# B products of the state space stage issued later, and list addresses computed between the expert selections

## The chip, the cores and the metric

One Trainium2 chip, of which the kernel uses one core. The metric is device microseconds for one execution; the kernel before took 1758.97 us (median of three runs, 1758.9 to 1761.51). The engines run side by side and wait for each other through semaphores: TensorE (PE; its weight loads are PEld), VectorE (DVE), ScalarE (ACT), GpSimd (POOL) and SyncE (SP), whose queue starts most transfers.

## The reference, cut to what matters

One decoder layer over 512 tokens of width 1024, float32 throughout:

```python
proj = h @ w_in[l]                       # u, q, k, v, indexer, merge gates
y_ssm = s5_branch(u, ...)                # 32 groups x 16 channels, 64 complex states, a scan over 512 positions
y_att = dsa_branch(...) @ w_attn_proj    # 8 heads, each query keeps 128 keys chosen by an indexer
mix = (g_ssm * y_ssm + g_att * y_att) @ w_o
h = layer_norm(ALPHA * h + mix, ...)
# experts
top_val, top_idx = lax.top_k(h @ w_router + b_router, 4)     # 4 of 32
# every expert: swiglu(x @ w_up + b_up) @ w_down + b_down, times the token's gate, summed over the 4
h = layer_norm(ALPHA * h + ffn, ...)
```

## The kernel before, in words

Every engine has one list of instructions in an order written out by hand; a `wait_ge` holds the whole list of its engine. Two stretches of these lists are touched.

**The state space stage.** The 32 groups are 16 blocks of 128 complex states (j = 0 to 15), taken in pairs. `bu(p)` (line 1474) is TensorE's B product of pair p: eight matmul records with 32 rows, into four PSUM banks. It waits until VectorE has taken the pair before it out of these banks (`s_bufree >= 2 * p`, which the fourth product of block 2p - 1 gives, line 1032). `s5(j)` on VectorE is twelve instructions (lines 1029 to 1045): four products with sines and cosines, two sums, two scans, four products; the last gives `s_st`. `ymm(q)` (line 1488) is the C product of four blocks and waits for `s_st >= 4 * q + 4`. Between them TensorE computes the tiles of the input projection (`tile`, line 1442 for most, 1423 for v, eight products of 128x128 by 512 each, shown as 16 records). Which product stands where is given by two tables over the tile index i of the loop at line 1497, and within one i the C product comes first:

```python
bu_at = {1: 1, 4: 2, 7: 3, 10: 4, 13: 5, 15: 6, 18: 7}
y_at = {6: 0, 12: 1, 17: 2}
```

After tile i = 20 TensorE goes on with `dots(0)` (line 1524), the first indexer products, which wait for `s_bufree >= 16`: the fourth product of the last block, j = 15. Gate tiles (line 1515) and further dots follow, until attention begins at `qk` (line 1556). A tile is copied out by ScalarE (`take`, line 738), in one list with its sines (`trigs`).

**The routing stage.** For each of four tiles t of 128 tokens: `w_out(t)` on TensorE, layer norm on VectorE (lines 1168 to 1182), transposes and router product (`route`, lines 1626 to 1640; ScalarE copies the transposes, line 860), the selection on VectorE (lines 1187 to 1204; ScalarE's two exponentials stand in the middle), `place(t)` (each token's position within its expert), then on VectorE `first_addresses(t)`: positions, the marks of the rows of expert 0 (`in_first`) and four list addresses for each token. GpSimd's `write_first(t)` writes the tokens' numbers with four indirect DMAs (line 586) to the list `first_list`. When all 16 writes have landed (`s_scat`) SyncE loads the list as `slots` (line 460), and only then issues the weight loads beyond the eighth part; VectorE waits for `slots` at line 1302, in front of its split `lo(-1, 7)`. `first_rows(t)` (line 1665) sums the rows of expert 0 straight into PSUM, a tile at a time, so that the first expert can begin before any list is read.

**The first expert** is `up_part(-1, p + 4, p)` for p = 0 to 7: three products for each of four banks (lines 1715 to 1717), of a weight part that SyncE loads, ScalarE rounds (`hi`, line 832) and VectorE takes the rest of (`lo`, line 1163). Part p needs `lo(-1, p + 4)`. Behind p = 1 stand the products of the first two tiles' gated biases (line 1694), whose sums VectorE takes in `sums` (line 1255) after `lo(-1, 7)`. The remaining experts run in a loop over blocks of 96 rows.

Of the kernel before, what the change touches and what calls it, by code (L numbers as in the profile page):

```python
# [16 lines left out]
ACT = mybir.ActivationFunctionType  # L17
ALU = mybir.AluOpType
# [7 lines left out]
P = 128  # L26
# [59 lines left out]
def build(nc, a, out):  # L86
# [14 lines left out]
    with ExitStack() as ctx:  # L101
# [555 lines left out]
        def _(act):  # L657
# [182 lines left out]
            for t in range(TT):  # L840
                act.wait_ge(s_var, TT + t + 1)
                s.activation(rsx[:, t, 0:1], mvx[:, t, 1:2], ACT.Sqrt, bias=eps[:, 0:1]).then_inc(s_rstd, 1)
                if t == 1:
                    act.wait_ge(s_bs, 1)
                    step(s.activation(bias3[third, :], braw_b[third, :], ACT.Copy))
                    s.activation(brem[third, :], bias3[third, :], ACT.Copy).then_inc(s_bc, 1)
                if t == 2:
                    step(s.activation(bias3[second, :], braw_b[second, :], ACT.Copy))
                    act.wait_ge(s_bs, 2)
                    s.activation(bias3[third, :], braw_b[third, :], ACT.Copy).then_inc(s_b3l, 1)  # L850
                if t == 3:
                    for c in range(4, 6):
                        hi(-1, c)
                act.wait_ge(s_h1, t + 1)
                act.dma_start(h1_rows.rearrange("(t p) d -> p t d", p=P)[:, t, :], h[:, t, :]).then_inc(s_h1row, 16)
                for r in range(2):
                    act.wait_ge(s_h1T, 2 * t + r + 1)
                    if t > 0:
                        act.wait_ge(s_lgt, t)
                    s.activation(hT1[:, 4 * r:4 * r + 4, :], ps[6 + r][:, :].rearrange("p (k q) -> p k q", k=4),  # L860
                                 ACT.Copy).then_inc(s_h1e, 1)
                act.wait_ge(s_v8, t + 1)
                s.activation(all_exp[:, t, :], lg[:, :], ACT.Exp, bias=gneg[:, 0:1])
                s.activation(gates[:, t, :], rt8[:, t, 0:TOPK], ACT.Exp, bias=gneg[:, 0:1],
                             accum_out=gsum[:, 0:1]).then_inc(s_ge, 1)
            def T_hi(dst, half, job, bank):

                act.wait_ge(s_tr, job + 1)
                s.activation(dst[:, 4 * half:4 * half + 4, :].rearrange("p k t -> p (k t)"), ps[bank][:, 0:4 * BLK],
                             ACT.Copy).then_inc(s_thi, 1)  # L870
# [10 lines left out]
            s.activation(gdT, ps[1][0:NE, :], ACT.Copy).then_inc(s_gdTe, 1)  # L881
# [54 lines left out]
        def _(dve):  # L936
# [209 lines left out]
            def first_addresses(t):  # L1146

                dve.wait_ge(s_pos, t + 1)
                step(d.tensor_copy(pos[:, t, :], ps[1][:, 0:NE]))
                d.tensor_scalar(in_first[:, t, :], tcol[:, 0:BLK], pos[:, t, 0:1], chosen[:, t, 0:1], ALU.is_equal,  # L1150
                                ALU.mult).then_inc(s_inf, 1)
                ad, picked = adw[:, t, 0, :], adw[:, t, 1, :]
                step(d.scalar_tensor_tensor(ad, pos[:, t, :], float(NE), tcol[:, 0:NE], ALU.mult, ALU.add))
                for k in range(TOPK):
                    step(d.scalar_tensor_tensor(picked, tcol[:, 0:NE], rif[:, t, k:k + 1], ad, ALU.is_equal, ALU.mult,
                                                accum_out=addr[:, t, k:k + 1]))
                d.tensor_copy(addr_i[:, TOPK * t:TOPK * t + TOPK], addr[:, t, :]).then_inc(s_adr, 1)
                dve.wait_ge(s_adr, t + 1)
# [8 lines left out]
            for t in range(TT):  # L1167
# [15 lines left out]
                if t > 0:  # L1183
                    first_addresses(t - 1)
                if t == TT - 1:
                    lo(-1, 4)
# [18 lines left out]
            first_addresses(TT - 1)  # L1205
# [90 lines left out]
            for half in range(2):  # L1296
                T_lo(x_lo, x_hi, half, half, 2 + half)
            lo(-1, 5)
# [3 lines left out]
            dve.wait_ge(s_slots, 16)  # L1302
            next_token(1)
            for c in range(7, 15):
                lo(-1, c)
                if c == 7:
                    dve.wait_ge(s_h1row, 16 * TT)
                    sums(0)
# [79 lines left out]
        def _(pe):  # L1388
# [105 lines left out]
            bu_at = {1: 1, 4: 2, 7: 3, 10: 4, 13: 5, 15: 6, 18: 7}  # L1494
# [131 lines left out]
            def route(t):  # L1626
                pe.wait_ge(s_h1, t + 1)
                for r in range(2):
# [5 lines left out]
                    ins.then_inc(s_h1T, 1)  # L1634
                pe.wait_ge(s_h1e, 2 * t + 2)
# [7 lines left out]
            def place(t):  # L1643

                pe.wait_ge(s_chosen, t + 1)
                if t > 0:
                    pe.wait_ge(s_adr, t)
# [5 lines left out]
            for t in range(TT):  # L1653
# [3 lines left out]
                if t > 0:  # L1657
                    route(t - 1)
# [12 lines left out]
            place(TT - 2)  # L1671
# [3 lines left out]
            first_rows(0)  # L1675
            first_rows(1)
            route(TT - 1)
# [8 lines left out]
            for t in range(TT):  # L1686
                ins = tr(ps[1][0:NE, P * t:P * t + P], all_exp[:, t, :], ident[:, :])
# [72 lines left out]
            pe.wait_ge(s_adr, TT)  # L1760
            pe.wait_ge(s_gdTe, 1)
            for p in range(8):
                up_part(-1, p + 4, p)
                if p == 1:
                    pe.wait_ge(s_bias, 64)
# [57 lines left out]
```

## Time and profile before

| | us |
|---|---|
| median of 3 runs | 1758.97 (1758.9 to 1761.51) |
| profiled execution | 1764.82, span 1763.10 |
| PE busy | 1686.9 (96%) |
| DVE busy | 1499.1 (85%) |
| ACT busy | 1063.4 (60%) |
| POOL busy | 467.5 (27%) |
| mean granted TensorE clock | 0.973 of full |

In the timeline a row is a start, a time, an engine, a line of the kernel, the operation, out<-in with shapes, and how many instructions are merged into it; in brackets stands how long the engine was idle before it and whose event ended this. An idle engine costs something only where the chain of waits runs through it.

### The profile page before, as it was taken

The page shows a single profiled execution, that of the slowest core. Times are in us where ns is not written, and L with a number is a line of the kernel's source. Part 1 is how long each engine was busy: PE and PEld are TensorE (multiplying, and loading weights), DVE is VectorE, ACT ScalarE, POOL GpSimd, SP SyncE. Part 2 cuts the span into 40 slices and gives each one's busy share as a digit, 9 for nine tenths or more (in the row PEclk, how much of TensorE's full clock was granted, in tenths as well). Part 3 has the DMA queues.
Part 4 walks back from the last instruction along what each step waited for, and adds up shares of the span by engine and source line. Part 5 has one row for each costly group of instructions (what it writes and reads, how often), then busy time and mean ns, then how long its engine had stood idle before and what let it go on. Part 6 is the DMA issues. An engine that isn't in the chain of part 4 may idle for free.

```text
span 1763.1 us, 22201 instructions
## 1 busy us (share of the span) xinstructions
PE 1686.9 (96%) x7129; PEld 1107.8 (63%) x7129; DVE 1499.1 (85%) x1710; ACT 1063.4 (60%) x1016; POOL 467.5 (27%) x298
## 2 busy tenths in 40 slices
PE   5899999999997999999999999999999999999996
PEld 2333344476576577777777777777777777777763
DVE  5999877555568799999999999999999999999995
ACT  4332222365445477777777777777777777777771
POOL 4855000064334111223121212222222212121210
PEclk9999899998998899999999999999999999999998
DMA  5111122110316789999999999999999999999973
GB/s 172 48 51 48 48 76 92 58 48 39 120 45 227 304 308 369 368 366 366 368 382 358 368 365 378 361 365 360 373 365 369 364 371 374 363 355 373 382 293 104
DMA packets 91901, 464.76 MB, mean 264 GB/s; under 512 B 21289, under 2 KB 21405, under 8 KB 42616
## 3 DMA queue, kind: packets, MB, share of 16 engines
q1 hardware_dynamic: 80240, 441.67, 65.9%
q0 software_dynamic: 9776, 18.41, 4.3%
q10 hardware_dynamic: 1848, 4.24, 0.7%
q8 instruction: 17, 0.28, 0.1%
q14 instruction: 20, 0.16, 0.0%
HBM read 454.15 MB, written 18.53 MB: 268 GB/s over the span
## 4 chain that ended last, share of the span: by engine, by line
PE 87%; DVE 9%; ACT 2%; issue 1%; DMA 0%; ACTq 0%; DVEq 0%
PE ps L1715 20%; PE ps L1717 20%; PE ps L1716 20%; PE ps L1515 6%; PE ps L1701 3%; PE ps L1442 2%; PE ps L1437 2%; PE ps L1723 2%; PE ps L1423 2%; PE ps L1431 1%; PE ps L1623 1%; PE ps L1622 1%; PE ps L1621 1%; PE ps L1576 1%; PE ps L1433 1%
## 5 line engine op out<-in xcount | busy, mean ns | idle before, releaser
L1163 DVE TENSOR_TENSOR w_lo<-raw,w_hi 128x2048 fp32r<-128x2048 f32 x384 | 874.1, 2287 | 76.3 <-ACT w_hi L832 76.2
L832 ACT ACTIVATE w_hi<-raw 128x2048 fp32r<-128x2048 f32 x384 | 737.0, 1920 | 244.6 <-PE ps L1717 244.2
L1715 PE MATMUL ps<-w_hi,x_hi 128*96 128x512 f32 x1024 | 415.9, 406 | 0.0
L1717 PE MATMUL ps<-w_lo,x_hi 128*96 128x512 f32 x1024 | 404.7, 395 | 0.0
L1716 PE MATMUL ps<-w_hi,x_lo 128*96 128x512 f32 x1024 | 404.4, 395 | 0.0
L1715 PEld LDWEIGHTS ps<-w_hi,x_hi 128*96 128x96 f32 x1024 | 169.3, 165 | 67.5 <-issue 1.5
L1717 PEld LDWEIGHTS ps<-w_lo,x_hi 128*96 128x96 f32 x1024 | 166.7, 163 | 71.1 <-issue 0.2
L1715 PE MATMUL ps<-w_hi,a_hi 128*96 128x512 f32 x512 | 204.6, 400 | 5.7 <-DVE a_lo L1261 5.7
L1716 PEld LDWEIGHTS ps<-w_hi,x_lo 128*96 128x96 f32 x1024 | 167.0, 163 | 64.0 <-issue 0.2
L1716 PE MATMUL ps<-w_hi,a_lo 128*96 128x512 f32 x512 | 201.8, 394 | 0.0
L604 POOL DMA_INDIRECT gate_now<-gate_rows,row_now x32 | 79.8, 2495 | 458.8 <-DVE tok_out L1291 443.7
L1717 PE MATMUL ps<-w_lo,a_hi 128*96 128x512 f32 x512 | 201.5, 394 | 0.0
L612 POOL DMA_INDIRECT sum_rows<-far,tok_out x31 | 77.2, 2489 | 335.7 <-ACT far L918 335.7
L1442 PE MATMUL ps<-ring 128*128 128x512 f32 x256 | 120.1, 629 | 2.5 <-ACT ring L686 2.0
L1515 PE MATMUL ps<-ring 128*128 128x512 f32 x256 | 111.5, 595 | 0.0
L1715 PEld LDWEIGHTS ps<-w_hi,a_hi 128*96 128x96 f32 x512 | 83.0, 162 | 39.2 <-issue 5.8
L1717 PEld LDWEIGHTS ps<-w_lo,a_hi 128*96 128x96 f32 x512 | 83.1, 162 | 36.3
L1716 PEld LDWEIGHTS ps<-w_hi,a_lo 128*96 128x96 f32 x512 | 83.3, 163 | 33.4
L1442 PEld LDWEIGHTS ps<-ring 128*128 128x128 f32 x256 | 50.8, 202 | 71.6 <-issue 69.3
L596 POOL DMA_INDIRECT scr<-h_rows,tok_now x32 | 70.5, 2205 | 81.3 <-DVE tok_now L1285 74.3
L1515 PEld LDWEIGHTS ps<-ring 128*128 128x128 f32 x256 | 48.2, 190 | 61.5 <-issue 61.2
L918 ACT ACTIVATE far<-ps,gate_now 96x512 f32<-96x512 f32 x64 | 40.3, 678 | 42.7 <-PE ps L1717 42.7
(323 smaller groups left out, 2034.6 us busy)
## 6 DMA issues: line engine op xcount, KB each, us to landing
raw<-in_w_up SPq DMA_DIRECT2D x256, 1024.0 KB, 8.0
raw<-in_w_down SPq DMA_DIRECT2D x128, 1024.0 KB, 9.4
ring<-in_w_in SPq DMA_DIRECT2D x9, 2048.0 KB, 7.8
ring<-in_w_glu SPq DMA_DIRECT2D x4, 1024.0 KB, 6.3
ring<-in_w_o SPq DMA_DIRECT2D x2, 2048.0 KB, 11.7
h<-in_x SPq DMA_DIRECT2D x4, 512.0 KB, 4.9
ring<-in_w_attn_proj SPq DMA_DIRECT2D x1, 2048.0 KB, 8.9
h_rows<-h ACTq DMA_DIRECT2D x4, 512.0 KB, 3.6
```

Source lines behind the costliest of these rows:

```text
L596: g.indirect_dma_start(xg[:, :], None, h1_rows, bass.IndirectOffsetOnAxis(ap=tok_now[:, 0:1], axis=0), bounds_check=last_tok, oob_is_err=F ...
L604: g.indirect_dma_start(gate_now[:, :], None, gate_rows, bass.IndirectOffsetOnAxis(ap=row_now[:, 0:1], axis=0), bounds_check=last_row, oob_ ...
L612: g.indirect_dma_start(sum_rows, bass.IndirectOffsetOnAxis(ap=tok_out[:, 0:1], axis=0), ysb.rearrange("p a b -> p (a b)"), None, bounds_ch ...
L832: s.activation(hi_of(c)[:, :], raw_of(c), ACT.Copy).then_inc(s_hi, 1)
L918: s.activation(ysb[:, r, :], ps[4 + r][0:BLK, :], ACT.Copy, scale=gate_now[:, 0:1]).then_inc(s_ysb, 1)
L1163: d.tensor_tensor(lo_of(c)[:, :], raw_of(c), hi_of(c)[:, :], ALU.subtract).then_inc(s_lo, 1)
L1442: ins = mm(o[:, :], w[:, k, c:c + P], hT[:, k, :], start=k == 0, stop=k == KD - 1)
L1515: ins = mm(ps[n % 2][:, :], gate_weights(g)[:, k, :], hT[:, k, :], start=k == 0, stop=k == KD - 1)
L1701: ins = tr(ps[bank][:, BLK * k:BLK * k + BLK], cols(k), ident[0:BLK, 0:BLK])
L1715: mm(o, xh, hi_of(c)[:, col], start=start, stop=False)
L1716: mm(o, xl, hi_of(c)[:, col], start=False, stop=False)
L1717: return mm(o, xh, lo_of(c)[:, col], start=False, stop=stop)
```

## The change

Five edits, in the diff below, cut where a loop body is only made into a function:

- `bu_at`: the third pair comes one tile later (4 to 5), the seventh two (15 to 17), the last one (18 to 19).
- VectorE: `norm1(3)` moves in front of `first_marks(1)` and `choose(2)`; the addresses of tiles 1 and 2 are computed together, behind `choose(2)`, those of tile 3 behind the x splits; each time by five instructions over all choices and tiles, in place of six for a tile. `lo(-1, 4)` moves behind the last marks, and the wait for `slots` behind `lo(-1, 7)`.
- ScalarE: `std(3)` moves in front of the exponentials of tile 2, the split `hi(-1, 4)` in front of those of tile 3.
- TensorE: the router's transposes and products of tile 3 move up, around `place(2)`; `place` waits for `s_inf` (marks) and no longer for `s_adr` (addresses).
- The gates' transposes go to bank 4 in place of bank 1, and their wait moves from in front of the first expert to behind p = 1; the wait for `s_adr >= TT` goes.

```diff
...
+            std(2)
+            step(s.activation(bias3[second, :], braw_b[second, :], ACT.Copy))
+            act.wait_ge(s_bs, 2)
+            s.activation(bias3[third, :], braw_b[third, :], ACT.Copy).then_inc(s_b3l, 1)
+            rows_off(2)
+            keep_hT1(2)
+            std(3)
+            gate_exps(2)
+            rows_off(3)
+            keep_hT1(3)
+            hi(-1, 4)
+            gate_exps(3)
+            hi(-1, 5)
...
-            def first_addresses(t):
+            def first_marks(t):
                 dve.wait_ge(s_pos, t + 1)
                 step(d.tensor_copy(pos[:, t, :], ps[1][:, 0:NE]))
                 d.tensor_scalar(in_first[:, t, :], tcol[:, 0:BLK], pos[:, t, 0:1], chosen[:, t, 0:1], ALU.is_equal,
                                 ALU.mult).then_inc(s_inf, 1)
-                ad, picked = adw[:, t, 0, :], adw[:, t, 1, :]
-                step(d.scalar_tensor_tensor(ad, pos[:, t, :], float(NE), tcol[:, 0:NE], ALU.mult, ALU.add))
-                for k in range(TOPK):
-                    step(d.scalar_tensor_tensor(picked, tcol[:, 0:NE], rif[:, t, k:k + 1], ad, ALU.is_equal, ALU.mult,
-                                                accum_out=addr[:, t, k:k + 1]))
-                d.tensor_copy(addr_i[:, TOPK * t:TOPK * t + TOPK], addr[:, t, :]).then_inc(s_adr, 1)
-                dve.wait_ge(s_adr, t + 1)
+            def first_addresses(t0, t1):
+                shape = [P, t1 - t0, TOPK, NE]
+                ad = adw[:, t0:t1, 0, :]
+                picked = part_lo[:, 0:(t1 - t0) * TOPK * NE].rearrange("p (t k e) -> p t k e", k=TOPK, e=NE)
+                step(d.scalar_tensor_tensor(ad, pos[:, t0:t1, :], float(NE),
+                                            tcol[:, 0:NE].unsqueeze(1).to_broadcast([P, t1 - t0, NE]), ALU.mult, ALU.add))
+                step(d.tensor_tensor(picked, tcol[:, 0:NE].unsqueeze(1).unsqueeze(1).to_broadcast(shape),
+                                     rif[:, t0:t1, 0:TOPK].unsqueeze(3).to_broadcast(shape), ALU.is_equal))
+                step(d.tensor_tensor(picked, picked, ad.unsqueeze(2).to_broadcast(shape), ALU.mult))
+                step(d.reduce_sum(addr[:, t0:t1, :], picked, AXL.X))
+                d.tensor_copy(addr_i[:, TOPK * t0:TOPK * t1], addr[:, t0:t1, :].rearrange("p t k -> p (t k)"))\
+                    .then_inc(s_adr, t1 - t0)
+                dve.wait_ge(s_adr, t1)
...
+            norm1(0)
+            choose(0)
+            norm1(1)
+            first_marks(0)
+            first_addresses(0, 1)
+            choose(1)
+            norm1(2)
+            norm1(3)
+            first_marks(1)
+            choose(2)
+            first_marks(2)
+            first_addresses(1, TT - 1)
+            choose(3)
+            first_marks(3)
+            lo(-1, 4)
...
             for half in range(2):
                 T_lo(x_lo, x_hi, half, half, 2 + half)
+            first_addresses(TT - 1, TT)
             lo(-1, 5)
             lo(-1, 6)
             tables()
             final = dve.value_load(etab_i[0:1, NB:NB + 1], min_val=NE - 1, max_val=NB - 2)
-            dve.wait_ge(s_slots, 16)
-            next_token(1)
             for c in range(7, 15):
                 lo(-1, c)
                 if c == 7:
+                    dve.wait_ge(s_slots, 16)
+                    next_token(1)
                     dve.wait_ge(s_h1row, 16 * TT)
                     sums(0)
...
-            bu_at = {1: 1, 4: 2, 7: 3, 10: 4, 13: 5, 15: 6, 18: 7}
+            bu_at = {1: 1, 5: 2, 7: 3, 10: 4, 13: 5, 17: 6, 19: 7}
...
                 if t > 0:
-                    pe.wait_ge(s_adr, t)
+                    pe.wait_ge(s_inf, t)
...
-            place(TT - 2)
             pe.wait_ge(s_wofree, 6)
             for half in range(2):
                 mm(ps[2 + half][:, 0:4 * BLK], ones_b[:, :], none_b[:, :], start=True, stop=False)
             first_rows(0)
+            route_T(TT - 1)
+            place(TT - 2)
+            route_lg(TT - 1)
             first_rows(1)
-            route(TT - 1)
             first_rows(2)
             place(TT - 1)
             first_rows(3)
@@ -1684,7 +1731,7 @@
 
...
-                ins = tr(ps[1][0:NE, P * t:P * t + P], all_exp[:, t, :], ident[:, :])
+                ins = tr(ps[4][0:NE, P * t:P * t + P], all_exp[:, t, :], ident[:, :])
...
-            pe.wait_ge(s_adr, TT)
-            pe.wait_ge(s_gdTe, 1)
             for p in range(8):
                 up_part(-1, p + 4, p)
                 if p == 1:
+                    pe.wait_ge(s_gdTe, 1)
                     pe.wait_ge(s_bias, 64)
                     gated_biases(0)
```

## Rows read from the trace of the kernel before

**Rows 1.** The page: busy time of TensorE, and the chain by engine.

```profile
PE 1686.9 (96%) x7129; PEld 1107.8 (63%) x7129; DVE 1499.1 (85%) x1710; ACT 1063.4 (60%) x1016; POOL 467.5 (27%) x298
...
PE 87%; DVE 9%; ACT 2%; issue 1%; DMA 0%; ACTq 0%; DVEq 0%
```

**Rows 2.** Timeline of TensorE, state space stage: start us, us, instructions, idle before.

```profile
59.72 20.87 PE L1442 MATMUL ps<-ring 128*128 128x512 f32 x48
84.67 3.08 PE L1474 MATMUL ps<-uT,ring 32*128 32x512 f32 x8 [4.09 <-DVE scr L1032]
...
124.28 7.11 PE L1442 MATMUL ps<-ring 128*128 128x512 f32 x16 [0.44 <-ACT wi L734]
132.14 1.99 PE L1474 MATMUL ps<-uT,ring 32*128 32x512 f32 x8 [0.75 <-ACT ring L738]
...
160.54 14.00 PE L1442 MATMUL ps<-ring 128*128 128x512 f32 x32
179.83 3.79 PE L1474 MATMUL ps<-uT,ring 32*128 32x512 f32 x8 [5.28 <-DVE scr L1032]
...
210.22 1.99 PE L1474 MATMUL ps<-uT,ring 32*128 32x512 f32 x8
212.13 14.00 PE L1423 MATMUL ps<-ring 128*128 128x512 f32 x32
```

**Rows 3.** Chain of waits: the C product of blocks 8 to 11.

```profile
199.66 3.57 PE ps L1488 x32
```

**Rows 4.** Busy time by stretch: time, PE, PEld, DVE, ACT, POOL, clock, DMA, GB/s.

```profile
84.67:92.24 7.57, 7.57 (x14) 2.91 (x15) 7.40 (x6) 0.66 (x2) 6.42 (x5) 0.55 0.00 0
179.83:187.84 8.01, 8.01 (x13) 3.08 (x14) 7.70 (x10) 1.16 (x3) 0.00 (x0) 0.50 0.00 0
226.07:349.63 123.56, 123.56 (x337) 53.29 (x336) 84.00 (x189) 29.86 (x48) 1.53 (x4) 1.00 0.22 77
```

**Rows 5.** Timeline of VectorE, state space stage.

```profile
131.31 0.69 DVE L1032 TENSOR_TENSOR scr<-ps,scr 128x512 f32<-128x512 f32 x1
...
186.59 0.69 DVE L1029 TENSOR_TENSOR scr<-ps,scr 128x512 f32<-128x512 f32 x1
...
212.25 0.69 DVE L1029 TENSOR_TENSOR scr<-ps,scr 128x512 f32<-128x512 f32 x1 [5.24 <-PE ps L1474]
...
224.21 0.69 DVE L1032 TENSOR_TENSOR scr<-ps,scr 128x512 f32<-128x512 f32 x1
```

**Rows 6.** Timeline of TensorE, routing and first expert.

```profile
541.48 1.07 PE L1632 MATMUL ps<-ident,h 128*128 128x128 f32 x8
...
569.12 1.03 PE L1723 MATMUL ps<-bias,pick 96*96 96x512 bf16 x4 [2.49 <-ACT scr L881]
...
589.60 0.39 PE L1715 MATMUL ps<-w_hi,x_hi 128*96 128x512 f32 x1
```

**Rows 7.** Timeline of VectorE, routing and first expert.

```profile
548.50 1.41 DVE L1171 SCALAR_TENSOR_TENSOR h<-h,ps 128x512 f32<-128x512 f32 x2
...
553.49 1.29 DVE L1181 SCALAR_TENSOR_TENSOR h<-h,rsx,gb 128x1024 f32<-128x1024 f32 x1
...
556.76 2.29 DVE L1163 TENSOR_TENSOR w_lo<-raw,w_hi 128x2048 fp32r<-128x2048 f32 x1
...
567.17 4.48 DVE L1163 TENSOR_TENSOR w_lo<-raw,w_hi 128x2048 fp32r<-128x2048 f32 x2
...
578.95 0.15 DVE L1284 COPY slot_now<-slots 96x1 int32<-96x1 int32 x1 [2.83 <-DMA slots<-first_list]
```

**Rows 8.** Timeline of GpSimd: four of the sixteen list writes.

```profile
544.48 0.98 POOL L586 DMA_INDIRECT first_list<-code,addr_i  x1 [7.83 <-DVE addr_i L1157]
...
557.50 2.41 POOL L586 DMA_INDIRECT first_list<-code,addr_i  x1 [8.18 <-DVE addr_i L1157]
...
567.27 5.24 POOL L586 DMA_INDIRECT first_list<-code,addr_i  x1 [0.31 <-issue]
572.81 0.98 POOL L586 DMA_INDIRECT first_list<-code,addr_i  x1 [0.30 <-issue]
```

More of the change, by code:

```diff
@@ L839, in _, with std, rows_off, keep_hT1 @@
             s.activation(brem, bias3[:, :], ACT.Copy).then_inc(s_bc, 1)
-            for t in range(TT):
+            def std(t):
                 act.wait_ge(s_var, TT + t + 1)
                 s.activation(rsx[:, t, 0:1], mvx[:, t, 1:2], ACT.Sqrt, bias=eps[:, 0:1]).then_inc(s_rstd, 1)
[L843 to L853, printed above, removed]
+            def rows_off(t):
                 act.wait_ge(s_h1, t + 1)
                 act.dma_start(h1_rows.rearrange("(t p) d -> p t d", p=P)[:, t, :], h[:, t, :]).then_inc(s_h1row, 16)
+            def keep_hT1(t):
                 for r in range(2):
@@ L861, in _, with gate_exps @@
                                  ACT.Copy).then_inc(s_h1e, 1)
+            def gate_exps(t):
                 act.wait_ge(s_v8, t + 1)
@@ L865, in _ @@
                              accum_out=gsum[:, 0:1]).then_inc(s_ge, 1)
+            std(0)
+            rows_off(0)
+            keep_hT1(0)
+            gate_exps(0)
+            std(1)
+            act.wait_ge(s_bs, 1)
+            step(s.activation(bias3[third, :], braw_b[third, :], ACT.Copy))
+            s.activation(brem[third, :], bias3[third, :], ACT.Copy).then_inc(s_bc, 1)
+            rows_off(1)
+            keep_hT1(1)
+            gate_exps(1)
+            std(2)
[11 more added lines that the diff above has]
+            hi(-1, 5)
             def T_hi(dst, half, job, bank):
@@ L880, in _ @@
             act.wait_ge(s_gdT, 1)
-            s.activation(gdT, ps[1][0:NE, :], ACT.Copy).then_inc(s_gdTe, 1)
+            s.activation(gdT, ps[4][0:NE, :], ACT.Copy).then_inc(s_gdTe, 1)
             def sigm(t, c):
@@ L1166, in _, with norm1 @@
             dve.wait_ge(s_gb2, 32)
-            for t in range(TT):
+            def norm1(t):
                 for r in range(2):
@@ L1182, in _, with choose @@
                     .then_inc(s_h1, 1)
[L1183 to L1186, printed above, removed]
+            def choose(t):
                 dve.wait_ge(s_lgt, t + 1)
@@ L1204, in _ @@
                 dve.wait_ge(s_gd, t + 1)
-            first_addresses(TT - 1)
+            norm1(0)
[13 more added lines that the diff above has]
+            lo(-1, 4)
             cnt, more, upto_e, t0 = rw[:, 0, :], rw[:, 1, :], rw[:, 2, :], rw[:, 3, :]
@@ L1624, in w_out, with route_T @@
                     ins.then_inc(s_wo, 1)
-            def route(t):
+            def route_T(t):
                 pe.wait_ge(s_h1, t + 1)
@@ L1634, in route, with route_lg @@
                     ins.then_inc(s_h1T, 1)
+            def route_lg(t):
                 pe.wait_ge(s_h1e, 2 * t + 2)
@@ L1657, in _ @@
                 if t > 0:
-                    route(t - 1)
+                    route_T(t - 1)
+                    route_lg(t - 1)
             def first_rows(t):
```

## The prediction, written before the changed kernel was run

> **What bounds the kernel now.** I read the page first, then the chain of waits in order of time, then the timelines of both changed stretches. On the page TensorE is busy 96% of the span and makes 87% of the chain [rows 1]: only what moves TensorE can move the end, and from the first expert on nothing in the change touches the loop. So there are two questions: when does TensorE reach the indexer products (`dots(0)`, 226.07 us), behind which it is busy in 123.56 of 123.56 us [rows 4], so that every delay there is passed on; and when does it get through the first expert.
>
> In the state space stage the reader is to see two waits of TensorE for VectorE, 4.09 us before the third pair and 5.28 us before the seventh [rows 2], each followed by a stretch at a granted clock of 0.55 and 0.50, that is for the most part or wholly at the lower of its two levels, 1.2 GHz [rows 4]. These the new tables go around. But VectorE is here nearly the equal of TensorE: from 42 to 212 us its only wait worth naming is 5.24 us, for the last pair [rows 5].
>
> **The state space stage, step by step.** Units: a tile is 7.0 us (14.00 for two), a B product 1.9 (210.22 to 212.13) [rows 2], a C product 3.6 [rows 3].
>
> Third pair. Today TensorE stops at 80.6 (59.72 + 20.87) until 84.67 and then works 7.57 us at 0.55. Tile i = 5 now fills the wait: 4.1 us and 7.57 x 0.45 = 3.4 us of lost clock go, a lead of 7.5 us. The fifth pair, which did not move, cannot use it. It needs block 7's fourth product, done at 131.31 + 0.69 = 132.0 [rows 5]; VectorE's pace does not come from the third pair, which it wants only at its next block but one. Today TensorE is there at 131.4 (124.28 + 7.11) and starts at 132.14 [rows 2]; then it would be there at 124 to 125 and wait 7 us. The lead is gone, and a wait longer than either of the two that cost clock stands in its place. I charge it what these lost: 3.4, or 8.01 x 0.5 = 4.0; taken 3.7, bounds 0 and 4.0. TensorE then runs 3.7 us late.
>
> Seventh pair. Today tile i = 15 ends at 160.54 + 14.00 = 174.5. It would end at 178.2, two more tiles at 192.3, and within i = 17 the C product stands first: 195.9, B product 197.8. The wait of 5.28 and its 4.0 go, but VectorE wants the pair at 186.59 [rows 5] and gets it at 197.8: it stands 11.2 us.
>
> Last pair. From 197.8 VectorE needs, up to block 15's fourth product, what it needed from 186.59 to 224.90 (224.21 + 0.69), less the 5.24 us wait, which goes [rows 5]: 33.1, with small waits inside of some 0.2 that go too, so 32.9. Result: 230.7. TensorE after the seventh pair has two tiles, the last pair and a tile (14.1 + 1.9 + 7.0): free at 220.9. It waits 9.8 us and begins `dots(0)` at 230.7 in place of 226.07: 4.6 us late. Behind so long a wait I charge half clock again, over the short dots (1.1 us more) and part of a gate tile (about 2.2): 3.3, bounds 0 and 4.0. Sum of the stage: **+7.9 us**, bounds +0.9 (no clock lost anywhere: 4.6 - 3.7) and +8.9.
>
> Queues: the moved products issue no DMA. SyncE's chunk loads hang on tile counts; the one needed next after the moved places, at the gate tiles, is 30 us away. ScalarE's sines for block 12 and later stand in its list behind tiles that now come some 4 us later; VectorE is 11 us late by then, which hides it.
>
> **The routing stage.** Today norm 3 starts on VectorE at 548.50 because selection 2 is in front, and ends at 554.78 (553.49 + 1.29) [rows 7]; the first expert starts at 569.12 behind a 2.49 us wait for the gates' copy [rows 6]. Then norm 3 starts with the last product of `w_out(3)`, which is out when TensorE turns to transposes at 541.48 [rows 6]; the first of its two additions can go before that, so it ends at about 541.6 + 6.3 - 0.7 = 547.2, 7.6 earlier. Behind it today are the addresses of tile 2, the split `lo(-1, 4)` (2.29), selection 3, marks and addresses 3, the marked rows, the x splits and the gates' wait: 14.3 us in all. Then: marks 1, selection 2 (about 3, my estimate), two tiles' addresses (about 1.8, as well), selection 3, marks, rows, x splits; the split, most address work and the gates' wait are out of it. I put it at the same 14.2: first expert at **561.4, 7.7 us early**. Bounds: 5, if the marked rows run at half clock; 9.5, if the first part of the expert also runs at full clock, which it does not today.
>
> This gain has a second door. The fifth part of the first expert starts today at 589.60, 20.5 us after the first [rows 6], and needs `lo(-1, 8)`, which stands on VectorE behind the wait for `slots`. Today this wait ends at 578.95 [rows 7], 6.1 us after the last of 16 list writes began (572.81) [rows 8]. Now the writes: four for tile 1 begin today at 544.48. Their addresses now come with tile 2's, at about 552.9, so 12 writes begin at about 553.7, 0.98 + 0.30 = 1.28 us apart [rows 8]: 15.4 us, 569.1. And they do not run free. The write of 557.50 took 2.41 us and ended at 559.91, 0.86 after the split that ran beside it (556.76 + 2.29); that of 567.27 took 5.24 and ended 0.86 after the two splits of 567.17 (+ 4.48) [rows 7, 8]. A write beside a split ends when the split has ended. In the new order the 12 writes meet `lo(-1, 4)` (from 557.4), 5 and 6 (from 562.6) and 7 (from 572): about 2.0 + 4.5 + 2.0 us more, less what falls into gaps. The last write would begin at 574.3 to 576.8, `slots` be there at 580.3 to 582.9. I take 581.5: 2.5 us later than today, though the expert starts 7.7 earlier. Then the tokens (0.3), the first sums (1.2) and `lo(-1, 8)` (2.3): 585.3. TensorE would be ready for part five at 561.4 + 20.5 = 581.9, or 1.8 earlier if its first products run at full clock. So it starts at 585.3, 4.3 earlier than today, after a wait of 3.4 to 5.2 us, behind which the clock may fall once more (0 to 4.0; taken 2.3). What is left: **-2.0 us**, bounds +0.5 and -9.5 (the writes unhindered).
>
> The Trainium skill (SBUF — State Buffer, Who interferes with whom) has a rule that speaks otherwise: a `tensor_tensor` of VectorE with both inputs in SBUF, which the splits are, contends with GpSimd's reads alone, and descriptor generation for GpSimd's DMAs was seen not to stall beside it. By it the writes would end at 569 and 7.5 of the gain or more stay. The two writes above contradict it in this trace.
>
> **Sum.** +7.9 - 2.0 = +5.9 us. Against the profiled execution before (1764.82, span 1763.10, so 1.7 us around it) that is 1770.7; the median of the runs lies 5.85 below that execution, so the forecast is 1758.97 + 5.9 = **1764.9**. 0.2% is 3.5 us, about what a measurement of this kernel tells from no change.
>
> **Rivals.** (A) *The list writes run free.* Place: GpSimd's twelve writes. Speaks for it: writes beside VectorE's small instructions take 0.98 us. Against: the two slow ones. (It is what the Trainium skill's rule above would give.) Price: `slots` at 574.3, the routing stage gives 7.7 to 9.5, so with +7.9 the sum is -1.6 to +0.2; not slower, 1758.2. It decides as soon as the last write begins before about 569.5. Chance 0.20, of it faster 0.07, same 0.13.
>
> (B) *The clock stays at 2.4 GHz in the new waits.* For it: only that the stages of the clock need not fall on the waits as before. Against: both waits of before cost it, and the new ones are longer. Price: +0.9 in the first stage, -4.3 in the second: 1755.6. Chance 0.13: faster 0.10, same 0.03.
>
> (C) *The second door eats the whole gain*: the clock falls behind part five's wait by 4.0 and `slots` comes at 583: routing +0.5 to -0.5, sum about +8.2: 1767.2. Chance 0.20, slower.
>
> (D) *The moves do not take effect*, because the gaps are closed by another wait at once. This is what I claim for the third pair and in part for the list; it is no case of its own.
>
> My own case has 0.47: slower 0.40, same 0.07. Together: faster 0.17, same 0.23, slower 0.60. Range for 8 in 10: 1757 to 1769; it takes in A and C, and leaves out most of B and the far end of C.
>
> **What would show it.** In the changed kernel's trace: no wait before the third and seventh pair, but one of 6 to 7 us before the fifth at 132, with a clock of 0.5 behind it; VectorE idle about 11 us before block 12; none before block 14; TensorE idle about 10 us before `dots(0)`, at 230 to 231. Then norm 3 done at 547, the first expert's first product at 561 plus the 8 us of delay from before, 12 list writes in one row with three long ones among them, VectorE waiting for `slots` behind `lo(-1, 7)`, and TensorE idle 3 to 5 us before part five. If `dots(0)` starts before 228, or the writes beside the splits take 1 us, the forecast is wrong.

## The result, and the profile after

The changed kernel took 1765.43 us (median of 10 runs, 1763.52 to 1768.58), the kernel before, timed beside it, 1760.99 us (10 runs). The ratio is 1.003, 95% interval 1.0018 to 1.0043, that is +5.3 us (+3.2 to +7.6); the two medians lie 4.4 apart. Forecast were 1764.9 us and +5.9. The sum is right. Its two terms, measured alone below, are off by 1.6 and 3.6 us in opposite directions, the first within its interval, the second just outside.

The page after (busy times, and the chain by engine), against [rows 1]:

```profile
PE 1683.0 (95%) x7129; PEld 1104.3 (62%) x7129; DVE 1501.3 (85%) x1685; ACT 1060.6 (60%) x1014; POOL 468.0 (26%) x298
...
PE 80%; DVE 14%; issue 2%; ACT 2%; DMA 1%; POOL 1%; ACTq 0%; DVEq 0%; POOLq 0%
```

VectorE's share of the chain rose from 9% to 14%: the state space stage now ends on it. TensorE's timeline there, the lines that answer to [rows 2] (line 1517 is the B product, 1485 and 1466 tiles, 1567 the indexer products, 1053 the fourth product of VectorE's block):

```profile
59.13 3.78 PE L1517 MATMUL ps<-uT,ring 32*128 32x512 f32 x8 [3.61 <-DVE scr L1053]
...
135.22 3.78 PE L1517 MATMUL ps<-uT,ring 32*128 32x512 f32 x8 [6.46 <-DVE scr L1053]
138.93 16.48 PE L1485 MATMUL ps<-ring 128*128 128x512 f32 x32
...
199.13 1.99 PE L1517 MATMUL ps<-uT,ring 32*128 32x512 f32 x8
201.05 14.00 PE L1466 MATMUL ps<-ring 128*128 128x512 f32 x32
214.98 1.99 PE L1517 MATMUL ps<-uT,ring 32*128 32x512 f32 x8
216.90 7.13 PE L1466 MATMUL ps<-ring 128*128 128x512 f32 x16
234.22 2.08 PE L1567 MATMUL ps<-kiT,qiT 64*128 64x256 f32 x8 [10.19 <-DVE scr L1053]
236.22 8.76 PE L1558 MATMUL ps<-ring 128*128 128x512 f32 x16
```

The waits before the third and the seventh pair are gone. In their place stands one of 6.46 us before the fifth and one of 10.19 us before the indexer products, which begin at 234.22 in place of 226.07. The first row is the second pair, ahead of every moved product: its wait is 3.61 us here, 0.92 in the profile of the kernel before, and from none to 3.67 in those of the other kernels, so it is no effect of the change. VectorE stood before block 12, for the seventh pair, and no longer before block 14:

```profile
201.22 0.69 DVE L1050 TENSOR_TENSOR scr<-ps,scr 128x512 f32<-128x512 f32 x1 [10.83 <-PE ps L1517]
```

Busy time by stretch, columns as in [rows 4] (the granted clock is the third number from the end). Behind each new wait, at least for part of the time, TensorE ran at 1.2 GHz, the lower of its two levels: 0.50 behind the one, 0.75 over the dots and the gate tile behind the other, 0.76 behind the wait in the first expert.

```profile
135.22:143.20 7.98, 7.98 (x13) 3.08 (x14) 7.78 (x7) 0.66 (x2) 6.83 (x5) 0.50 0.00 0
...
234.22:245.00 10.78, 10.78 (x28) 4.92 (x32) 8.29 (x12) 2.71 (x5) 0.00 (x0) 0.75 0.00 0
590.76:598.00 7.24, 7.24 (x20) 4.06 (x21) 7.24 (x5) 1.91 (x1) 0.55 (x1) 0.76 1.00 377
```

The routing stage, TensorE first (the lines for [rows 6]; `w_out(3)` ended at about 548.87, before at 541.45):

```profile
569.87 1.06 PE L1770 MATMUL ps<-bias,pick 96*96 96x512 bf16 x4 [1.01 <-DVE x_lo L1303]
590.76 0.47 PE L1762 MATMUL ps<-w_hi,x_hi 128*96 128x512 f32 x1 [3.35 <-DVE w_lo L1192]
612.10 1.93 PE L1770 MATMUL ps<-bias,pick 96*96 96x512 bf16 x4 [3.79 <-DVE x_lo L1303]
```

VectorE's splits and the copy behind the wait for `slots` ([rows 7]), and GpSimd's list writes ([rows 8]), of which there are twelve in one row from 561.26 to 579.34:

```profile
566.16 2.28 DVE L1192 TENSOR_TENSOR w_lo<-raw,w_hi 128x2048 fp32r<-128x2048 f32 x1
...
571.13 4.49 DVE L1192 TENSOR_TENSOR w_lo<-raw,w_hi 128x2048 fp32r<-128x2048 f32 x2
...
586.96 0.15 DVE L1326 COPY slot_now<-slots 96x1 int32<-96x1 int32 x1 [3.39 <-DMA slots<-first_list]
```

```profile
565.11 0.98 POOL L586 DMA_INDIRECT first_list<-code,addr_i  x1 [0.30 <-issue]
566.39 2.90 POOL L586 DMA_INDIRECT first_list<-code,addr_i  x1 [0.30 <-issue]
...
572.17 2.10 POOL L586 DMA_INDIRECT first_list<-code,addr_i  x1 [0.30 <-issue]
574.58 1.90 POOL L586 DMA_INDIRECT first_list<-code,addr_i  x1 [0.30 <-issue]
...
579.34 0.98 POOL L586 DMA_INDIRECT first_list<-code,addr_i  x1 [0.30 <-issue]
```

Measured from the end of `w_out(3)`, the first expert starts 6.7 us earlier than before (21.0 for 27.7), its part five 6.3 earlier (41.9 for 48.15), the loop over the other experts 4.6 earlier (63.2 for 67.8). From there to the end both kernels take the same (1154.7 and 1153.8).

### The profile page after: what moved, and what is told of

It reads as the page before. It is cut to its first block, busy times and chain, and to the rows that moved or that the text cites. A ratio compares the mean times of both kernels' runs of the same rounds, so it can differ in the third digit from the quotient of the medians.

```text
span 1766.8 us, 22174 instructions
## 1 busy us (share of the span) xinstructions
PE 1683.0 (95%) x7129; PEld 1104.3 (62%) x7129; DVE 1501.3 (85%) x1685; ACT 1060.6 (60%) x1014; POOL 468.0 (26%) x298
## 4 chain that ended last, share of the span: by engine, by line
PE 80%; DVE 14%; issue 2%; ACT 2%; DMA 1%; POOL 1%; ACTq 0%; DVEq 0%; POOLq 0%
PE ps L1762 18%; PE ps L1764 18%; PE ps L1763 18%; PE ps L1558 6%; PE ps L1485 3%; DVE w_lo L1192 3%; PE ps L1748 3%; PE ps L1480 2%; PE ps L1770 1%; PE ps L1474 1%; DVE scr L1058 1%; DVE scr L1059 1%; PE ps L1619 1%; PE ps L1476 1%; PE ps L1475 1%
```

## The experiments

Each was timed in five rounds beside the kernel before; the differences are against those runs, with the interval of the ratio times 1761 us. "Dots" is the start of the indexer products; "routing" is the time from the end of `w_out(3)` to the start of the loop; both come from the one profiled execution of each. The difference is taken from the ratio and can lie away from that of the medians, most in kernel 7, whose median is 4.8 us above.

| kernel | us against before | dots | routing |
|---|---|---|---|
| before | | 226.07 | 67.8 |
| changed | +5.3 (+3.2 to +7.6) | 234.22 | 63.2 |
| 1: new B places alone | +9.5 (+6.0 to +13.0) | 233.09 | 68.4 |
| 2: routing alone | -5.6 (-8.8 to -2.5) | 226.16 | 62.5 |
| 3: before, seventh pair at 16 | -2.6 (-5.3 to -0.2) | 217.88 | 68.4 |
| 4: as 2, tile 1's addresses early | -4.6 (-7.6 to -1.6) | 228.45 | 63.3 |
| 5: before, third pair at 5 | -0.4 (-3.2 to +2.6) | 227.66 | 69.0 |
| 6: as 2, two splits shortened | -4.8 (-7.6 to -1.9) | 225.81 | 60.5 |
| 7: before, seventh pair at 17 | +1.1 (-2.5 to +4.4) | 232.84 | 66.7 |
| 8: changed, B at 5, 7, 11, 13, 16, 18 | -6.0 (-9.0 to -3.0) | 225.19 | 62.8 |
| 9: as 2, seventh pair at 16 | -8.1 (-11.1 to -5.1) | 220.48 | 65.5 |
| 10: as 9, `slots` behind `lo(-1, 8)` | -13.4 (-17.8 to -9.0) | 219.31 | 61.1 |
| 11: changed, seventh pair at 16 | +3.0 (+0.7 to +5.5) | 228.34 | 62.7 |
| 12: changed, GpSimd held | +3.0 (+0.2 to +5.8) | 230.37 | 60.3 |

### 1 and 2: the two halves alone

```diff
-            bu_at = {1: 1, 4: 2, 7: 3, 10: 4, 13: 5, 15: 6, 18: 7}
+            bu_at = {1: 1, 5: 2, 7: 3, 10: 4, 13: 5, 17: 6, 19: 7}
```

> The kernel before with the new places of the B products alone, all of the routing as before. My theory (clock lost behind the new waits, the last pair late because the seventh comes late): the indexer products begin at about 234 instead of 226, as in the changed kernel, and nothing gives it back, so +7 to +10 us, 1.004 to 1.006 of before. Rival B (the new waits cost no clock): +0.9 us. A third theory, from the trace after: the 10.7 us by which the state space stage ends late are partly the first pair's 1.3 us chance, so +9 in the records but about +7 in the times.

Measured +9.5 us. Rival B (no clock lost) is out: +0.9 lies far below the interval, and the waits of the changed kernel are there again, 5.53 us before the fifth pair, at half clock, and 10.18 before the dots. The third theory, 1.3 us of chance from the first pairs, has no support in the trace: VectorE's fourth product of block 3 stood at 83.74 here, 83.76 in the changed kernel and 83.84 before. The second run has all of the change but this line.

> The changed kernel with the B products at their old places: the routing change alone. My prediction's term: -2.0 us (list writes hindered by the splits, part five waits for its split and loses clock behind that). The trace after, counted from the end of the last output product, had the loop's start 4.6 us nearer: then -4 to -5 us. Rival A (writes run free): -7.6 to -9.5. In its trace the 12 writes should show three to four long ones, each ending about 0.86 us after a split of VectorE, and TensorE should wait some 3 us before part five.

Measured -5.6 us: more than the forecast's -2.0, which lies just outside the interval. Rival A's -7.6 to -9.5 lie partly inside it, but its mechanism is not there: of the 12 writes three were long (2.15, 2.10, 1.90 us). TensorE waited 3.68 us before part five. The two halves add to +3.9, against +5.3 measured together.

### 3 and 7: the seventh pair, one place apart

```diff
-            bu_at = {1: 1, 4: 2, 7: 3, 10: 4, 13: 5, 15: 6, 18: 7}
+            bu_at = {1: 1, 4: 2, 7: 3, 10: 4, 13: 5, 16: 6, 18: 7}
```

> The kernel before with one number changed: the seventh pair behind tile 16 in place of 15, so that one tile fills TensorE's wait of 5.28 us there but the C product of tile 17 does not come in front. If the lateness of the changed kernel comes from putting two tiles and the C product before the seventh pair, this one gives VectorE the pair at most 2 us later than before, loses no clock there, and begins the indexer products 3 to 7 us earlier than before: -3 to -7 us. If a later seventh pair is harmful in itself, it ends 1 to 3 us slower.

> The kernel before with the seventh pair alone behind tile 17, so that two tiles and the C product stand in front of it. Theory (that place is what costs): TensorE ends these at about 192, the B product at 194, VectorE waits some 7 us before block 12, and the indexer products begin at about 227 to 228 where the kernel before has 226.07: the wait of VectorE has only moved, +0 to +3 us. Against the first run with 16 in its place this should be 4 to 9 us slower in the trace. If the C product in front costs nothing, it equals the run with 16.

The second has `17: 6`. With 16, VectorE never waits from 120 us to the dots, and TensorE's wait for the last products is 2.64 us:

```profile
179.70 1.99 PE L1474 MATMUL ps<-uT,ring 32*128 32x512 f32 x8
181.62 7.13 PE L1423 MATMUL ps<-ring 128*128 128x512 f32 x16
...
217.88 1.14 PE L1524 MATMUL ps<-kiT,qiT 64*128 64x256 f32 x8 [2.64 <-DVE scr L1032]
```

With 17, the C product of tile 17 stands in front of it, VectorE waits 10.81 us, and the dots begin 15.0 us later:

```profile
197.77 1.99 PE L1474 MATMUL ps<-uT,ring 32*128 32x512 f32 x8
199.68 7.13 PE L1423 MATMUL ps<-ring 128*128 128x512 f32 x16
212.54 3.78 PE L1474 MATMUL ps<-uT,ring 32*128 32x512 f32 x8 [5.73 <-DVE scr L1032]
```

Two more kernels with 16 (9 and 10) have the dots at 220.48 and 219.31. But not all of the 15.0 us comes from the seventh pair's place. Its wait ends with VectorE's fourth product of block 11, and this was already 4.2 us later in kernel 7 than in kernel 3, since in its profile the low clock behind the second pair lasted longer, no wait was left before the third, and VectorE's blocks were longer (the reason is under run 12). Kernel 3, then kernel 7:

```profile
177.29 0.69 DVE L1032 TENSOR_TENSOR scr<-ps,scr 128x512 f32<-128x512 f32 x1
```

```profile
181.48 0.69 DVE L1032 TENSOR_TENSOR scr<-ps,scr 128x512 f32<-128x512 f32 x1
```

Counted from the start of that product, the dots come after 47.1 us in the kernel before (178.99 to 226.07; 44.8 to 47.4 in the others with the seventh pair at 15), after 40.6 in all four kernels with the pairs at 16 and 18 (3, 8, 9, 10) and after 51.4 in all four with the seventh at 17 (the changed one, 1, 7, 12). In the trace, then, one tile saves 6.5 us, and two tiles with the C product cost 4.3. The times are -2.6 and +1.1 by the ratios, -1.8 and +4.8 by the medians. What else moves them is taken up below.

### 5 and 11: is the third pair at fault?

```diff
-            bu_at = {1: 1, 4: 2, 7: 3, 10: 4, 13: 5, 15: 6, 18: 7}
+            bu_at = {1: 1, 5: 2, 7: 3, 10: 4, 13: 5, 15: 6, 18: 7}
```

> The kernel before with the third pair alone behind tile 5 in place of 4. My steps say: the wait before the third pair goes, one of 6 to 7 us at half clock comes before the fifth, TensorE is 3.7 us late at 158; but tile 15 then ends when the seventh pair's operands are nearly there, so the wait of 5.28 us before the seventh pair and its lost clock go too, VectorE gets that pair before it asks for it, and the last pair comes some 3.5 us earlier than before: -3 to -4 us. Rival (the moved third pair is itself harmful, since its 3.7 us stay): +3 to +4 us.

Missed on both sides: no change (-0.4). Its trace has the wait of 6.45 us before the fifth pair, the wait before the seventh cut to 1.77, and still the dots at 227.66, since VectorE came to its fourth product of block 11 at 181.15, 2.2 us later than before.

In the changed kernel `17: 6` became `16: 6`:

> The changed kernel with one number undone by one: the seventh pair behind tile 16 in place of 17. If the place behind the C product is what made the state space stage late: VectorE's wait of 10.8 us before block 12 goes to under 2, one of 4 to 6 us comes before block 14 (the last pair stays behind tile 19), the indexer products begin at 226 to 230 in place of 234.2, and the time is 4 to 8 us below the changed kernel's 1765.4. If the third pair's move is the cause, it stays above 1762.

VectorE's wait of 10.8 us is gone, one of 6.13 us stands before block 14, for the last pair, and the dots begin at 228.34: the trace is as expected. The time went down only from 1765.43 to 1764.33 (each in its own group of runs; against before +3.0 for +5.3), less than the 4 to 8 us expected. It stayed above 1762, which the expectation had named as the sign that the third pair's move is the cause. Kernel 5 (-0.4) speaks against that, and so does kernel 8, which has the third pair at 5 too and lies at -6.0, where the routing alone is at -5.6.

A third suspect was never moved alone: the last pair, from 18 to 19. With the third pair alone at -0.4 and the seventh alone at +1.1, nothing adds up to kernel 1's +9.5. The four kernels that have 19 (the changed one, 1, 11, 12) cost 8.6 to 10.9 us more than the kernel with the same routing and the old places, and no kernel without it costs more than +1.1 (+4.8 by its median). In kernel 7 TensorE's wait of 5.73 us stands before the last pair and the dots follow at full clock; in the four it stands before the dots (5.77 to 10.19 us), and dots and gate tile behind it run slow. At the C product behind them that makes some 2 us (243.14 in kernel 1, 240.96 in kernel 7); whether the last pair's place is what costs the rest stays open.

### 12: GpSimd held

What kernels 1, 5 and the changed one have in common in the trace are longer blocks of VectorE. In the kernel before, the block from 96.32 to 106.09 us (fourth product to fourth product) takes 9.8 us, and GpSimd is idle meanwhile; with the third pair at 5 it took 11.7 us (changed), 12.6 (kernel 1), 12.1 (5), 12.6 (8) and 11.7 (11). The two scans in this block, before and in kernel 1:

```profile
98.50 1.22 DVE L1037 TENSOR_TENSOR_SCAN scr<-spw,scr 128x512 f32<-128x512 f32 x1
99.75 1.22 DVE L1038 TENSOR_TENSOR_SCAN scr<-spw,scr 128x512 f32<-128x512 f32 x1
```

```profile
98.40 2.31 DVE L1037 TENSOR_TENSOR_SCAN scr<-spw,scr 128x512 f32<-128x512 f32 x1
100.75 2.11 DVE L1038 TENSOR_TENSOR_SCAN scr<-spw,scr 128x512 f32<-128x512 f32 x1
```

And GpSimd's first instruction behind its pause, before and in kernel 1:

```profile
105.94 1.30 POOL L513 TENSOR_TENSOR v<-v,ring 128x512 f32<-128x512 f32 x1 [12.22 <-ACT part_lo L696]
```

```profile
98.35 1.28 POOL L513 TENSOR_TENSOR v<-v,ring 128x512 f32<-128x512 f32 x1 [4.73 <-ACT part_lo L696]
```

GpSimd waits for ScalarE's phase products of block 9 (the tenth of its sixteen rounds), and these stand in ScalarE's list behind the copy of a tile. Before, TensorE had stood 4.09 us in front of the third pair, that copy came at 103.97, and GpSimd was kept away from VectorE's scans. Filling the wait brought copy and GpSimd 7.6 us forward, onto the scans. (In kernels 6 and 7, which leave the third pair at 4, the low clock behind the second pair made TensorE late enough for no wait before the third, and this block took 11.7 us there too.) The twelfth run gives GpSimd one wait more:

```diff
                 pool.wait_ge(s_prod, 2 * j + 2)
+                if j == 8:
+                    pool.wait_ge(s_st, 5)
```

> The changed kernel with one wait added: GpSimd's phases of block 8 begin only when VectorE has finished block 4 (as they did by chance in the kernel before, at 105.94 us, since ScalarE stood in front of a late tile). Theory (GpSimd beside VectorE lengthens VectorE's blocks, and the moved third pair let it in early): VectorE's block 4 to 5 takes 9.8 us again instead of 11.7, the fifth B product starts 2 to 3 us earlier than 135.2, its wait before is 4 to 5 us instead of 6.46. The seventh pair hangs on TensorE's list and comes 2 to 3 us earlier too, and so do the indexer products: -1.5 to -3 us. If the contention only moves into the next block, all is the same within 0.5 us.

The expectation takes the row at 105.94 for block 8; it is block 9, and block 8's phases had begun at 85.48 before. So this run holds GpSimd one block earlier than the kernel before did:

```profile
100.88 1.28 POOL L515 TENSOR_TENSOR v<-v,ring 128x512 f32<-128x512 f32 x1 [16.87 <-DVE gb L1068]
```

VectorE's block took 9.8 us again, and so did the one ahead of it (before 12.5); the two behind them took 14.3 and 13.2 in place of 13.1 and 12.5. The fifth pair began at 131.32 instead of 135.22, the dots at 230.37 instead of 234.22. The wait before the fifth pair did not get shorter (6.75 us), since TensorE came earlier as well, after a shorter stretch of low clock behind the second pair. The contention does move on, but not all of it. As the cause of VectorE's longer blocks it is shown in the trace; the time (+3.0 against before, interval +0.2 to +5.8) does not tell it from the changed kernel.

### 4, 6 and 10: the list

Kernels 4 and 6 have the old places of the B products besides, kernel 10 those of kernel 9.

```diff
             first_marks(1)
+            first_addresses(1, 2)
             choose(2)
             first_marks(2)
-            first_addresses(1, TT - 1)
+            first_addresses(2, TT - 1)
```

> The routing change alone, but tile 1's addresses are worked out right behind its marks, before the second selection, and tile 2's behind its own. Four of the twelve writes go out some 5 us earlier. If the list (writes in a row, hindered by splits) is what holds part five of the first expert, its wait of 3.35 us goes and the run is 2 to 4 us faster than the routing change alone, less some 0.5 us for four more small instructions in front of the first expert's rows. If the list is not what holds it, the run is 0.5 us to 1 us slower than the routing change alone.

Missed: no gain against kernel 2. Eight writes ran free, but the last four wait for tile 3's addresses and start beside two splits (2.41 and 1.90 us), at 563.19; `slots` came 15.5 us after the first expert's start (kernel 2: 17.4), and TensorE still waited 2.78 us before part five. Counted from the end of `w_out(3)`, `slots` did not come earlier at all (39.2 us, kernel 2: 36.2), and the expert itself began later (23.6 for 18.7). Kernels with kernel 2's list range from 18.7 to 23.6 there as well. So this run does not tell what an earlier list is worth.

```diff
-            lo(-1, 5)
-            lo(-1, 6)
+            for c in (5, 6):
+                dve.wait_ge(s_hi, part_no(-1, c) + 1)
+                d.tensor_scalar(lo_of(c)[:, :], hi_of(c)[:, :], 0.0, None, ALU.mult).then_inc(s_lo, 1)
```

> The routing change alone, with the two splits of parts 5 and 6 replaced by an instruction of VectorE with one input and a scalar (the low halves become zero: that correction is left out). Same 128x2048 floats written. Theory: the long list writes come from VectorE's large instructions with two inputs in SBUF; then the two writes of 2.10 and 1.90 us become 0.98, the list's last write begins 2 us earlier or more, and so does the read of slots; if the one-input form is also faster than 2.28 us, VectorE's tables come earlier as well, but that changes nothing at part five. Time: -1 to -3 us against the routing change alone. If any large instruction of VectorE holds the writes, the long ones stay and the time is the same.

VectorE's two instructions, and the two writes beside them:

```profile
556.48 2.37 DVE L1343 TENSOR_SCALAR w_lo<-w_hi 128x2048 fp32r<-128x2048 f32 x2
```

```profile
556.24 1.59 POOL L586 DMA_INDIRECT first_list<-code,addr_i  x1 [0.30 <-issue]
558.14 1.56 POOL L586 DMA_INDIRECT first_list<-code,addr_i  x1 [0.31 <-issue]
```

One input in place of two, 1.19 us each in place of 2.28: the writes were still held, and the second ended 0.85 us after VectorE's second (558.85, 559.70). So two inputs are not what it takes; the hold gets shorter because the instruction does. The last write began 9.9 us after the expert's start instead of 10.8. The time did not fall below kernel 2's.

The tenth kernel leaves the list alone and changes who waits for it:

```diff
             for c in range(7, 15):
                 lo(-1, c)
-                if c == 7:
+                if c == 8:
                     dve.wait_ge(s_slots, 16)
                     next_token(1)
```

> The kernel of the run above with the wait for slots, the tokens and the first sums of VectorE one split later, behind the split of part eight, which part five of TensorE's products needs. If the list holds part five (second door), TensorE's wait of about 3.4 us there goes; it comes back at once if the gated biases of tile 2 wait for the first sums instead, or at the start of the loop, where TensorE waited 3.8 us for the gathered rows in every kernel so far: gain 0 to -3 us. If the wait before the loop grows by what part five gains, the list's way to the loop is the gather, and the time does not change.

TensorE has no wait before part five at all, where kernel 9, the same but for this line, waited 5.46 us. Kernel 9, then kernel 10:

```profile
556.46 1.06 PE L1770 MATMUL ps<-bias,pick 96*96 96x512 bf16 x4 [1.01 <-DVE x_lo L1303]
570.22 0.47 PE L1762 MATMUL ps<-w_hi,x_hi 128*96 128x512 f32 x1 [0.55 <-DVE w_lo L1192]
578.70 0.74 PE L1762 MATMUL ps<-w_hi,x_hi 128*96 128x512 f32 x1 [5.46 <-DVE w_lo L1192]
601.26 1.94 PE L1770 MATMUL ps<-bias,pick 96*96 96x512 bf16 x4 [3.75 <-DVE x_lo L1303]
```

```profile
553.73 1.06 PE L1770 MATMUL ps<-bias,pick 96*96 96x512 bf16 x4 [1.01 <-DVE x_lo L1303]
567.25 0.48 PE L1762 MATMUL ps<-w_hi,x_hi 128*96 128x512 f32 x1 [0.34 <-DVE w_lo L1192]
591.25 1.94 PE L1770 MATMUL ps<-bias,pick 96*96 96x512 bf16 x4 [5.20 <-DVE x_lo L1303]
```

From the expert's start to the loop it is 37.5 us for 44.8. The wait before the loop grew by 1.45 us, and from the loop's start to the end kernel 10 took 1156.3 us, kernel 9 1152.9 (the others up to 1154.7), with a wait of 1.1 us for gathered rows in it. So of the 4.4 us won up to the loop the trace gives 3.4 back behind it. Its median, 1749.24 us, is 4.9 below kernel 9's, timed in the same rounds. The second door was real as a wait of TensorE; how much of the 4.9 us is its doing the traces do not settle, since kernel 10's unchanged stretch between dots and `w_out(3)` was 4.4 us shorter too.

### 8 and 9: the best places with the routing change

Kernel 8 has all the new places filled by hand: `{1: 1, 5: 2, 7: 3, 11: 4, 13: 5, 16: 6, 18: 7}`.

> The changed kernel with other places for the B products: behind tiles 1, 5, 7, 11, 13, 16, 18. The third pair keeps its new place, the fifth goes one tile later so that a tile fills the wait of 6.46 us that the changed kernel has there, the seventh stands one tile earlier, before the C product. From the theory of the state space stage: no wait over 3 us there, no half clock, indexer products at 217 to 220, so -6 to -9 us for the stage and -5.6 for the routing as measured alone: 1746 to 1750 us. If the lateness cannot be taken out by places (VectorE the bound), it is no better than the routing change alone, 1754.6.

No better than kernel 2. The wait before the fifth pair is gone, VectorE does not wait from 120 us on, and yet the dots begin at 225.19, behind 3.35 us of waiting for it: from 84.5 to 173.5 us its blocks take 12.5 to 13.2 us each, none of them 9.8, with GpSimd beside it in every one.

> The routing change with the seventh pair behind tile 16 and all other B products as before. Parts measured alone: routing -5.6, the seventh pair at 16 -2.6 in the times (-8.2 in the trace, up to the indexer products). If both hold and add: 1761 - 8 = 1753, and in the trace the indexer products at 218 to 220 with no wait of VectorE over 1 us between 42 and 217 us. If the trace of the run with 16 was a lucky one (VectorE's blocks beside GpSimd were shorter there), the indexer products begin at 222 to 226 and the time is that of the routing change alone.

As expected: 1754.17 us, -8.1, the sum of its parts. With kernel 10's line it is the version that beats both, 1749.24 us, 0.9924 of before (0.9899 to 0.9949).

## Why the prediction came out right, and what in it was wrong

**The fifth pair's wait: right, its length partly by luck, and 3 us late.** Forecast were a wait of 6 to 7 us at 132 and half clock; it is 6.46 us at 135.2. Both of its ends had moved: TensorE was there at 128.8 and not at 124 to 125, after its wait before the second pair and the low clock behind it, and VectorE was 3.1 us later than forecast. The step "VectorE's pace does not come from the third pair" failed. By data it does not. By who works beside it, it does: kernel 1, without low clock behind the second pair, has the block of 12.6 us, and run 12 put the fifth pair back to 131.3. The clock behind the wait cost 4.3 us (1.8 in the B product, 2.5 in the two tiles), forecast 3.7.

**The seventh pair: right.** Forecast 197.8 and 11.2 us of waiting; measured 201.05 for the end of the B product and 10.83. The traces of runs 3 and 7 show that the place behind the C product is what costs up to the dots, and that one place earlier would have gained.

**The last pair and the dots: 3.5 us too early.** Forecast 230.7, measured 234.2, for the same reason as above. **The clock behind it: right.** Forecast 3.3; the dots and the gate tile took 0.9 and 1.6 us more than at full clock, 2.6 in all.

**The stage: +7.9 forecast, +9.5 alone (+6.0 to +13.0).** The trace has +8.15 at the dots and +10.7 at the C product behind them. The interval takes in the forecast, and the single moves do not add up to the +9.5 (see run 11).

**The routing: -2.0 forecast, -5.6 alone.** The step that failed is the length of the row of writes. It began where forecast (12.4 us after `w_out(3)`; forecast 12.3), but the splits added 4.0 us to it (18.08 from first to last start, 14.08 = 11 x 1.28 without), where the forecast had the last one begin 20.6 to 23.1 us after the first: a write that starts inside a split waits only for the rest of it, and its own 0.98 us are part of that; and the row was over before `lo(-1, 7)`. The forecast was off the other way in the path behind it: from the last write's start to VectorE's copy of `slots` it took 6.1 us from one row; here it was 7.6, and 6.1 to 9.0 over all kernels. So `slots` came 0.6 us later than before, from `w_out(3)`, not 2.5. Part five started 6.3 us earlier, not 4.3, and 1.7 of this went again up to the loop (forecast 2.3). One trace is a weak measure of this stage: up to the loop the changed routing took 60.3 to 65.5 us in six kernels, the old one 66.7 to 69.0 in five. The means, 62.8 and 68.1, lie 5.2 apart, which fits the -5.6.

**Rival A** falls by its mechanism, since the writes did not run free: three took 2.90, 2.10 and 1.90 us for 0.98. The Trainium skill (SBUF — State Buffer, Who interferes with whom) has it that descriptor generation was seen not to stall beside a `tensor_tensor`; these three writes show the contrary. The same section of the Trainium skill names the one-input `tensor_scalar` among those that can take the shared ports, and with that kernel 6 agrees (1.59 and 1.56 us). **B** falls by run 1, **C** by run 2.

So the net was right by two errors of opposite sign, and in so far by luck: +1.6 in the first stage, which its interval does not tell from nothing, and -3.6 in the second. The halves alone add to +3.9 and not +5.3; the intervals cover that too.

**Open.** The times follow the dots only in part (kernels 3, 7, 11, 12). Between the dots and the end of `w_out(3)`, where the tables of the B products change no instruction, the profiled executions took from 306 us (kernels 5 and 8) to 318 (kernel 12), before 315.3. The clock is the whole difference: TensorE's idle time in the stretch is 12.8 us each time, only its busy time varies. Before, then kernel 5:

```profile
226.07:541.41 315.34, 302.58 (x1154) 183.87 (x1154) 193.18 (x397) 127.14 (x222) 90.40 (x68) 0.96 0.19 68
```

```profile
227.66:533.50 305.84, 293.06 (x1154) 178.42 (x1153) 190.87 (x397) 126.02 (x222) 91.46 (x68) 0.99 0.20 69
```

Much of this is chance in each execution, for it is there within one kernel. Of the 101 runs of the kernel before that were timed beside these experiments, the 31 with a mean granted clock of 0.973 or less have a median of 1765.65 us, the 24 with 0.977 or more one of 1758.1. Whether the way the stage before ends shifts the odds as well, as the four kernels with the last pair at 19 would suggest, stays open.

## What to carry to other kernels

Before filling a wait, write down where each later product of the same queue lands, and what other engines the wait was holding back: here TensorE's pause kept ScalarE, and through it GpSimd, off VectorE's scans. Move by the smallest step past the wait, and not past the next long item (the C product): in the traces one tile gained where two lost. Move one product at a time, too: here three moved together cost more than two of them alone, and the third was never tried alone. Where one engine's list has a wait for a slow transfer, look what stands behind it that somebody else needs; with that one item moved ahead the median was 4.9 us lower, though the traces put part of that down to the clock elsewhere. Two attempts to bring the list itself forward showed no gain, but neither brought it more than 2 us nearer to the expert's start.

## What the runs showed of the hardware that was not expected

- A scan of 128x512 on VectorE takes 1.22 us alone and 2.1 to 2.3 beside GpSimd's float instructions, a block of twelve instructions 9.8 us or up to 14.3.
- A list write of GpSimd beside a large VectorE instruction ends about 0.85 us after it, whether that has two inputs (2.28 us) or one (1.19 us). One that had begun 0.25 us ahead of such an instruction took its usual 0.98 us (changed kernel, 570.88).
- An unchanged stretch of about 310 us took 306.0 to 318.0 us in profiled executions of kernels that differ only ahead of it (kernels 8 and 12), with the same 12.8 us of idle time and a granted clock of 0.99 and 0.95.
